# Rounding a chunk's staged rows in two halves, so that two engines start their remainders at different times

## The reference

```python
def modulate_in(x, mod, k, g):
    return rms_norm(x, g) * (1.0 + mod[:, None, 3 * k + 1]) + mod[:, None, 3 * k]

def gated_residual(x, out, mod, k, g):
    return x + mod[:, None, 3 * k + 2] * rms_norm(out, g)
```

## Time and profile before

| | us |
|---|---|
| three timed runs | 2083.16, 2088.36, 2088.58 |
| their median | 2088.36 |
| the profiled execution | 2084.32 |
| its span, first to last instruction | 2082.6 |

### The profile page before, as it was taken

One profiled execution on the slowest core, in us unless ns is written; L12 is line 12 of the kernel. 1 busy time (PEld: TensorE's weight loads), 2 busy tenths in 40 slices (PEclk: granted clock), 3 DMA queues, 4 the chain that ended last, 5 costly groups with the idle time before them and its releaser, 6 DMA issues.

```text
span 2082.6 us, 30152 instructions
## 1 busy us (share of the span) xinstructions
PE 1964.7 (94%) x11823; PEld 1744.7 (84%) x11823; DVE 1194.7 (57%) x1778; ACT 923.5 (44%) x1566; POOL 708.9 (34%) x515
## 2 busy tenths in 40 slices
PE   6689999999999989999999998899999979899998
PEld 3479998799998877799987875799987867799986
DVE  2557772466535565777733863777733684777722
ACT  2344442444545544544433424544433544544432
POOL 0033324332234445333243741323333431323332
PEclk8889999999999999999999999999999989999999
DMA  9853336543330135544354673544364513244342
GB/s 400 342 220 128 122 112 240 184 123 122 116 132 16 36 119 219 223 149 122 123 211 157 237 201 155 200 147 127 122 207 157 214 56 112 81 145 128 123 125 78
DMA packets 80316, 324.31 MB, mean 156 GB/s; under 512 B 9008, under 2 KB 17712, under 8 KB 66608
## 3 DMA queue, kind: packets, MB, share of 16 engines
q1 hardware_dynamic: 78496, 319.42, 44.5%
q10 hardware_dynamic: 1680, 2.96, 0.4%
HBM read 317.24 MB, written 5.10 MB: 155 GB/s over the span
## 4 chain that ended last, share of the span: by engine, by line
PE 83%; DVE 5%; ACT 4%; issue 2%; POOL 2%; DMA 1%; DVEq 0%; ACTq 0%; POOLq 0%
PE pair L1719 17%; PE pair L1721 17%; PE pair L1720 17%; PE pair L1753 7%; PE pair L1755 7%; PE pair L1754 7%; PE pair L1867 3%; DVE x L1263 2%; PE pair L1961 1%; ACT junk L861 1%; DMA mod_more<-in_w_mod 1%; PE pair L1907 1%; PE pair L1690 1%; DVE wk L1254 1%; PE pair L1872 1%
## 5 line engine op out<-in xcount | busy, mean ns | idle before, releaser
L710 POOL TENSOR_TENSOR w_lo<-raw,w_hi 128x512 fp32r<-128x512 f32 (+1 forms) x375 | 584.4, 1560 | 1139.9 <-ACT w_hi L833 1139.6
L1719 PE MATMUL pair<-h_hi,w_hi 128*128 128x386 f32 (+1 forms) x2008 | 687.7, 342 | 17.7 <-POOL h_lo L717 17.4
L1721 PE MATMUL pair<-h_hi,w_lo 128*128 128x386 f32 (+1 forms) x2008 | 683.1, 340 | 0.0
L1720 PE MATMUL pair<-h_lo,w_hi 128*128 128x386 f32 (+1 forms) x2008 | 682.5, 340 | 0.0
L1197 DVE TENSOR_TENSOR w_lo<-raw,w_hi 128x512 fp32r<-128x512 f32 x339 | 416.0, 1230 | 311.4 <-ACT w_hi L833 311.3
L833 ACT ACTIVATE w_hi<-raw 128x1024 fp32r<-128x1024 f32 x375 | 392.7, 1050 | 262.1 <-PE pair L1755 226.2
L1719 PEld LDWEIGHTS pair<-h_hi,w_hi 128*128 128x128 f32 (+1 forms) x2008 | 380.6, 190 | 23.4 <-POOL h_lo L717 21.1
L1720 PEld LDWEIGHTS pair<-h_lo,w_hi 128*128 128x128 f32 (+1 forms) x2008 | 381.3, 190 | 0.9
L1721 PEld LDWEIGHTS pair<-h_hi,w_lo 128*128 128x128 f32 (+1 forms) x2008 | 380.5, 189 | 0.3
L1321 DVE SCALAR_TENSOR_TENSOR acc<-pair,taps,acc 128x385 f32<-128x385 f32 x176 | 108.9, 619 | 212.8 <-ACT acc L920 212.8
L920 ACT ACTIVATE acc<-pair,taps 128x386 f32<-128x386 f32 x176 | 117.2, 666 | 236.5 <-PE pair L1721 236.5
(11 more groups left out here) (279 smaller groups left out, 2216.3 us busy)
## 6 DMA issues: line engine op xcount, KB each, us to landing
raw<-in_ffn_in SPq DMA_DIRECT2D x176, 512.0 KB, 3.5
raw<-in_ffn_out SPq DMA_DIRECT2D x88, 512.0 KB, 3.6
mod_raw<-in_w_mod SPq DMA_DIRECT2D x32, 1024.0 KB, 7.1
mod_base<-in_w_mod SPq DMA_DIRECT2D x31, 1024.0 KB, 7.9
mod_more<-in_w_mod SPq DMA_DIRECT2D x22, 1024.0 KB, 19.5
raw<-in_ssd_conv SPq DMA_DIRECT2D x32, 512.0 KB, 3.5
raw<-in_ssd_z SPq DMA_DIRECT2D x16, 512.0 KB, 3.5
raw<-in_ssd_out SPq DMA_DIRECT2D x16, 512.0 KB, 3.8
```

The lines of the kernel that those rows point to most:

```text
L710: pool.tensor_tensor(w_lo[:, m % SLOTS, 0:w], raw[:, m % SLOTS, 0:w], w_hi[:, m % SLOTS, 0:w].bitcast(F32), ALU.subtract).then_inc(w_low_p ...
L1719: ten.matmul(to, wh, h_hi[:, k, cols], start=k == 0, stop=False, skip_group_check=True)
L1720: ten.matmul(to, wh, h_lo[:, k, cols], start=False, stop=False, skip_group_check=True)
L1721: ins = ten.matmul(to, wl, h_hi[:, k, cols], start=False, stop=k == KD - 1, skip_group_check=True)
```

## The change

ACT rounds blocks 0 to 3 as soon as it has staged them itself, and blocks 4 to 7 when DVE has. Each of the two counts on `h_hi_ready`, which so goes to two per chunk: POOL waits for the first, DVE for the second. The three functions are POOL's, ACT's and DVE's, in this order.

```diff
             def unit_low(t, c):
                 e, cols = event(t, c), slice(AT[c], AT[c] + P)
-                pool.wait_ge(h_hi_ready, e + 1)
+                pool.wait_ge(h_hi_ready, 2 * e + 1)
...
             def unit_high(t, c):
                 e, cols = event(t, c), slice(AT[c], AT[c] + P)
                 act.wait_ge(stage_act, e + 1)
+                act.activation(h_hi[:, 0:4, cols], stage[:, e % 2, 0:4, :], ACT.Copy).then_inc(h_hi_ready, 1)
                 act.wait_ge(stage_dve, e + 1)
-                act.activation(h_hi[:, :, cols], stage[:, e % 2, :, :], ACT.Copy).then_inc(h_hi_ready, 1)
+                act.activation(h_hi[:, 4:, cols], stage[:, e % 2, 4:, :], ACT.Copy).then_inc(h_hi_ready, 1)
...
             def unit_low(t, c):
                 e, cols = event(t, c), slice(AT[c], AT[c] + P)
-                vec.wait_ge(h_hi_ready, e + 1)
+                vec.wait_ge(h_hi_ready, 2 * e + 2)
```

## The result

| | before | changed |
|---|---|---|
| timed runs | 4 | 4 |
| median, us | 2086.35 | 2074.37 |
| lowest to highest, us | 2083.16 to 2088.58 | 2073.41 to 2076.17 |
| profiled execution, us | 2084.32 | 2075.24 |
| its span, us | 2082.6 | 2073.5 |

The ratio of the changed kernel to the one before is 0.995, with a 95% interval of 0.9935 to 0.9965: it is faster by 7.3 to 13.6 us. The forecast was 2078 us, with a gain of 7.9. By the medians the gain is 12.0 us, from profile to profile 9.1.

A forecast was written before the change was run, and what follows sets the result against it. TensorE's late starts at seven transitions, mostly behind POOL's last subtraction, were taken to bound the kernel. Gains of 1.35 + 1.43 + 1.4 + 1.07 + 0.15 + 1.07 + 1.4 = 7.9 us off 2086.1 gave 2078, range 2072 to 2084.

The forecast's parts named there:

- The roundings: ACT's 21 whole roundings become 42 halves of 0.62 us; each pair costs 0.08 us more, hidden by ACT's waits.
- Chunk 0: At t = 1 POOL starts at 406.91 instead of 407.35, so DVE's residual and what follows come 0.44 us earlier.
- Chunk 1: POOL goes ahead of DVE, also with w_lo; DVE stages chunk 2 0.16 us later; over 10 us, this step failed.
- Chunk 2: At t = 1 POOL subtracts before DVE, which is now last; TensorE's load comes at 419.15, a gain of 1.43 us.
- t = 3 and 5: Transitions where POOL alone makes the weight chunk: it starts about 1.0 us earlier, and the load gains 1.07 us each.
- t = 0, 2 and 6: Transitions forecast to gain 1.35 us at t = 0, and 1.4 us each at t = 2 and 6.
- t = 4: Transition where TensorE's own modulation products end last; at most 0.28 us to be had, 0.15 taken.
- The sum: The gains of TensorE's start at the seven transitions, added up to 7.9 us.
- The clock: TensorE's granted clock, low after t = 1 and 6, was left as it is in the sum, with no gain counted.
- Little: Rival: what POOL gains DVE loses, or other work sets some starts; 4 to 5 us remain, about 2082; chance 0.31.
- More: Rival: DVE's w_lo first at chunk 1, or clock held after t = 1 or 6; 10.3 to 12 us; chance 0.12.
- Slower: Rival: TensorE's clock falls at t = 2 to 5, costing 14 us against 7.9; about 2092; chance 0.03.

The follow-up runs named there:

- f1: The changed kernel, but at chunk 1 POOL waits for both halves, so that DVE goes first there; median 2076.27 us.
- e1: The changed kernel run once more, unaltered; median 2073.82 us.
- e4: The changed kernel with halves at chunks 0 and 1 alone, chunk 2 rounded whole; median 2085.64 us.
- e3: The changed kernel with halves at chunk 2 alone, chunks 0 and 1 rounded whole as before; median 2075.94 us.
- g3: The kernel before, whole roundings, but at chunk 0 POOL's subtraction waits until DVE has made its own; median 2079.79 us.
- f4: The kernel before, whole roundings, but at chunks 1 and 2 POOL's subtraction waits for the end of DVE's; median 2085.56 us.

## Why the prediction held, point by point

- **The roundings.** 42 in place of 21, the groups by form give 628 and 620 ns (forecast 620), the second starting 0.52 us behind the first as reckoned (405.17, 405.69).
- **Chunk 0.** POOL starts 0.69 us behind the rounding's start, and residual(2) takes 1.52 us, forecast 1.5. The first half of chunk 1 starts 5.90 us behind that of chunk 0 (411.07 in the timeline), forecast 5.89.
- **Chunk 1.** POOL goes first and POOL's w_lo ahead of DVE's, as forecast. Each hand-over cost some 0.05 to 0.1 us more than my rows gave: DVE stages chunk 2 9.97 us behind chunk 0's rounding, forecast 9.80, and under the 10 at which the step would have failed. f1 puts the price of this order at 0.5 us at each of three transitions.
- **Chunk 2.** POOL 1.18 us, forecast 1.2; DVE's end to the weight load 0.33, forecast 0.35. From rounding to load it is 13.05 us at t = 1, forecast 12.93: 1.32 us saved for 1.43.
- **t = 3 and 5.** 0.92 us each for 1.07. DVE goes behind POOL as reckoned, and again ends a little later than reckoned: 0.55 us behind POOL's end, for which I had 0.48 (1151.73 and 1151.18). Timeline at the end of t = 3, answering to the earlier trace rows:

```profile
1150.00 1.18 POOL L717 TENSOR_TENSOR h_lo<-stage,h_hi 128x512 fp32r<-128x512 f32 x1
1150.05 1.68 DVE L1291 TENSOR_TENSOR h_lo<-stage,h_hi 128x512 fp32r<-128x512 f32 x1 [0.98 <-ACT h_hi L884]
...
1152.06 0.19 PEld L1720 LDWEIGHTS pair<-h_hi,w_hi 128*128 128x128 f32 x1 [1.62 <-POOL h_lo L717]
```

- **t = 0, 2 and 6.** In the two profiles 1.31 and 1.26, 1.30 and 1.29, 1.35 and 1.32 us, forecast 1.35, 1.4 and 1.4.
- **t = 4.** I took 0.15 us; it was -0.15 and 0.58 in two profiles of the same kernel, with TensorE's own products last in both.
- **The sum.** 7.0 and 7.6 us in the two profiles for 7.9. The mechanism was right, and its term for the hand-overs some 0.1 us short at each end.
- **The clock.** The sum put it at nothing, and that was too little. Behind t = 1 it now stays at the upper level; four us from the load on, first before, then changed (busy us of PE, PEld, DVE, ACT and POOL, then the granted clock, third from the end):

```profile
420.60:424.60 4.00, 3.99 (x15) 4.00 (x16) 3.90 (x8) 0.00 (x0) 2.92 (x2) 0.62 0.40 121
```

```profile
418.20:422.20 4.00, 3.95 (x22) 3.98 (x23) 3.67 (x6) 0.86 (x1) 3.48 (x2) 1.00 0.30 78
```

That is 0.38 x 4 = 1.5 us, an estimate, and the stretch from this load to transition 2 is 1.4 us shorter. But this stretch moves by itself, from 413.6 to 417.5 us over the thirteen profiles, though its work is the same in all. The nine that kept the clock at its beginning average 414.9 us and differ by 3.9, the four that lost it average 415.8; what moves it I haven't settled. Behind t = 6 the clock is seen more clearly. Seven of the thirteen profiles had 0.57 to 0.65 in the four us from the load on and 287.8 to 288.1 us from there to the end, six had 0.50 and 288.6 to 289.3. The kernel before is one of the six; of the changed kernel's two profiles each went its way, changed and e1:

```profile
1785.70:1789.70 4.00, 3.99 (x15) 4.00 (x16) 3.33 (x5) 0.82 (x1) 3.41 (x2) 0.65 0.29 77
```

```profile
1782.90:1786.90 4.00, 3.94 (x12) 3.97 (x13) 3.35 (x5) 0.84 (x1) 3.44 (x2) 0.50 0.28 73
```

So the 1.3 us that the changed kernel's profile saved there came by luck: its load came 3.6 us behind the last product before it, e1's 3.3. The rest of the 2.1 us: 0.7 saved ahead of t = 6 and 0.25 at the start, 0.5 and 1.0 lost behind t = 0 and 4.
- **The time.** 2078 was 3.8 us too high, by two things. The base of 2086.1 was the mean of four runs, two of them at 2088; in the 49 runs beside the experiments the kernel before has medians of 2084.08 to 2084.53, so 1.8 us are the base. The other 2.0 are the gain: about 9.9 us against such a base, of which the transitions are 7.0 to 7.6 and the stretches between them the rest.
- **The rivals.** Little: not what happened, but its reason is real, as e4 shows (at t = 1, 2 and 6 the halves at chunks 0 and 1 lose 0.3 us). More: the part on the clock came true at t = 1, and by the time alone, 2074.37 us, its 2075 lies nearer than the forecast's 2078. The gains from profile to profile, 9.1 us and in e1 10.5, lie on both sides of the border at 10: the transitions went as in the forecast, and part of what came on top is this rival's. The part on DVE's weight remainder didn't, and f1 shows what it would have given: 0.5 us at three transitions, not 0.8. Slower: the clock didn't fall at t = 2, 3 or 5 in any profile of the changed kernel.

The forecast's path through all three chunks was right in its sum, but not evenly in what carries it: the halves at chunks 0 and 1, two thirds of the edit, bring 1.4 us of 5.8, by e3.

## What to carry to other kernels

When two engines can't run a pair of operations together, write down the row of these operations at the stage's end, in order: it can't get shorter than the sum of its operations, so what counts is how early it can start and that nothing on the critical path stands behind an operation that is not. Here it paid more to hold POOL back at chunk 0, where its work wasn't due (3.75 us at five transitions, g3), than to start it early there and at chunk 1 (0.2 us, e4); at chunk 2, where TensorE waits for it, the early start paid (4.4 us, e3). An edit's parts are best tried one by one even where the whole gains: here one chunk of three carried three quarters of it, and another held a loss that only a run of its own showed.

## What the runs showed of the hardware that was not expected

- The small size of DVE's operation did not spare it the wait: one of 128x1, 0.16 us by itself, took 0.82 us beside a subtraction of POOL's. The Trainium skill (SBUF — State Buffer, "SBUF: two separate sides") calls the port pair that the two share an exclusive lock, taken for the whole instruction by an operation of GpSimd, or by one of VectorE with two SBUF inputs against it. The rows agree: residual(2) is 1.28 us with POOL elsewhere and 1.52 to 2.28 beside it, and POOL's subtraction about 1.19 us when it comes first and up to 1.70 behind DVE's.
- Standing in wait for the other engine was cheaper than waiting for it on a semaphore: by an estimated 0.21 us at each hand-over from DVE to POOL (f4).
- TensorE's clock at t = 1 and 2, in thirteen profiles: behind 16 loads that came at most 1.6 us after the last product before them, the four us that follow had 1.00 each time. Behind ten that came 1.9 to 3.2 us after it, six fell to 0.57 to 0.64 and four stayed at 1.00. At t = 6 the load came 2.6 to 5.2 us after it, and the clock was at 0.50 to 0.65 in all thirteen; at t = 3 and 5, at most 2.1 us after it, 1.00 in all. So the shortest waits kept the clock here and longer ones often lost it. What decided among the ten isn't shown; the length of the wait did not, since 2.9 us kept it (f4) and 1.9 lost it (g3). The Trainium skill (TensorE: Matmul & The Clock Gate, Part 1) has the gate's monitor run freely, not in step with the kernel; four of ten being spared agrees with that, but doesn't prove it.
